# Linear attention's chunks placed between the key-block steps of the prompt attention, its exponents summed by TensorE

## The reference, cut to what matters

```python
def _fox_prompt(q, k, v, logf):            # prompt attention
    c = cumsum(logf)
    s = q @ k.T * scale + c[t] - c[s]       # causal
    return softmax(s) @ v

def _gla_chunk(S, inp):                     # one chunk of L tokens
    q, k, v, g = inp                        # g = log of the gates
    b = cumsum(g, axis=1)
    o_inter = (q * exp(b)) @ S
    A[t, s] = sum_k q[t, k] * k[s, k] * exp(b[t, k] - b[s, k])   # s <= t
    o = o_inter + A @ v
    S_new = exp(b_last) * S + (k * exp(b_last - b)).T @ v
```

## Time and profile before

| what | us |
|---|---|
| median of 3 runs (3704.17 to 3709.93) | 3708.62 |
| profiled execution, its own time | 3711.19 |
| its span, first to last instruction | 3709.5 |
| `fox_prompt` from its first instruction to the loop | 773.17 to 799.38 |
| `fox_prompt`'s loop | 799.4 to 1333.0 |
| `gla`'s first instruction, `merge`'s first | 1464.66, 1768.90 |

### The profile page before, as it was taken

The page is one execution under the profiler, slowest core; times in us unless marked ns, Lnnn a source line. Parts: engine busy times, 40 slices in busy tenths (PEclk is TensorE's granted clock), DMA queues, the critical chain, the costliest instruction groups (busy, mean ns, idle before and its releaser), DMA issues. The chain is left out here.

```text
span 3709.5 us, 47795 instructions
## 1 busy us (share of the span) xinstructions
PE 3229.8 (87%) x17920; PEld 2840.7 (77%) x17920; DVE 2089.8 (56%) x3141; ACT 835.2 (23%) x1455; POOL 649.7 (18%) x379
## 2 busy tenths in 40 slices
PE   5999999749999966566699699999998799999996
PEld 5999999625555535455477599999998699999995
DVE  5001112264444424798333378778776677787786
ACT  5111111223333311222222211111112211111112
POOL 0000000021212000565000322222223122222220
PEclk9999999869999978678799799999999799999997
DMA  4223121132221061222444411111112311111112
GB/s 108 69 69 113 54 69 51 32 83 52 47 57 41 12 186 60 65 76 63 127 143 129 125 46 45 45 49 47 45 45 89 113 46 45 45 45 45 51 39 87
DMA packets 246611, 255.76 MB, mean 69 GB/s; under 512 B 38009, under 2 KB 207369, under 8 KB 240289
## 3 DMA queue, kind: packets, MB, share of 16 engines
q1 hardware_dynamic: 245193, 250.42, 23.4%
q10 hardware_dynamic: 1344, 4.36, 0.5%
HBM read 187.82 MB, written 66.92 MB: 69 GB/s over the span
## 5 line engine op out<-in xcount | busy, mean ns | idle before, releaser
L2086 PE MATMUL ps_ffn<-h,wsp_n 128*128 128x312 f32 (+1 forms) x6336 | 1057.6, 323 | 42.1 <-POOL h L1922 28.6
L2086 PEld LDWEIGHTS ps_ffn<-h,wsp_n 128*128 128x128 f32 x6336 | 1018.4, 189 | 48.3 <-issue 37.6
L2021 DVE TENSOR_TENSOR yacc<-ps_ffn,yacc 128x312 f32<-128x312 f32 (+1 forms) x1056 | 495.1, 514 | 222.2 <-PE ps_ffn L2101 222.2
L391 PE MATMUL ps_project<-hT,wsp 128*128 128x416 f32 x3000 | 580.1, 354 | 3.2 <-DVE wsp L335 3.2
L391 PEld LDWEIGHTS ps_project<-hT,wsp 128*128 128x128 f32 x3000 | 562.1, 189 | 12.0 <-issue 5.0
L2101 PE MATMUL ps_ffn<-aT,dsp 128*128 128x312 f32 (+1 forms) x3168 | 545.0, 321 | 9.0 <-DVE yacc L2021 9.0
L2101 PEld LDWEIGHTS ps_ffn<-aT,dsp 128*128 128x128 f32 x3168 | 508.5, 188 | 11.7 <-issue 8.9
L1917 POOL TENSOR_TENSOR wsp_n<-wraw_n,wsp_n 128x1024 fp32r<-128x1024 f32 x88 | 210.5, 2392 | 801.9 <-ACT wsp_n L1958 801.9
L2035 DVE RECIPROCAL silu<-silu 128x416 f32<-128x416 f32 x132 | 306.2, 2320 | 4.5
L833 PE MATMUL ps_fox<-pexp,va 128*65 128x512 f32 (+3 forms) x640 | 295.6, 544 | 5.4 <-ACT pexp L880 5.4
L1988 ACT ACTIVATE aT<-a 128x416 fp32r<-128x416 f32 x132 | 65.2, 494 | 1004.1 <-DVE a L2043 1004.1
(11 more groups left out here) (222 smaller groups left out, 3125.0 us busy)
## 6 DMA issues: line engine op xcount, KB each, us to landing
wraw_n<-in_w_gate_dram SPq DMA_DIRECT2D x44, 512.0 KB, 3.8
wraw_n<-in_w_up_dram SPq DMA_DIRECT2D x44, 512.0 KB, 3.8
draw<-in_w_down_dram SPq DMA_DIRECT2D x44, 512.0 KB, 3.6
qk_raw<-zT SPq DMA_DIRECT2D x32, 512.0 KB
zT<-zs SPq DMA_DIRECT2D x12, 1040.0 KB
wraw<-in_w_in_dram SPq DMA_DIRECT2D x24, 512.0 KB
x<-x2s SPq DMA_DIRECT2D x20, 416.0 KB
h2T<-hT_m SPq DMA_DIRECT2D x20, 416.0 KB
```

The costliest lines, as they stand in the source:

```text
L391: last = pe.matmul(ps[:, g, 0:BLK], wsp[:, b, s, k, :], hT[:, g * TPB:(g + 1) * TPB, v, k, :], start=m == 0, stop=m == 3 * KD - 1)
L2021: dve.tensor_tensor(y, ps[:, 4 + i, 0:FB[b] * TT], y, ALU.add).then_inc(added, 1)
L2086: last = pe.matmul(ps[:, 2 * q + s, 0:FB[b] * TT], wsp[:, par, s, w, k, :], h2[:, FB0[b]:FB0[b + 1], v, k, :], start=m == 0, stop=m == 3 * ...
```

## The change

The stage `gla` goes. Its work on the 17 chunks moves into the prompt attention's stage, now `attend`, and none of it stays on GpSimd except masks.

- `gates` keeps the tokens on the partitions: nine pairs of chunks of 128 tokens by 256 channels (the bias comes in with a row of ones). It makes no running sums. The logarithms are stored in a high and a low fp32r part, `glog`, 4.2 MB where `gsum` had 2.1 MB.
- The exponents of all levels are matmuls: `gh`, the loaded logarithms, against `within`, a constant matrix of zeros and ones that GpSimd builds in `attend` before anything else of it can run (42 mask selects where `gla` had 14).
- A chunk's work is cut into steps r = 0 to 21 (`chunk_step` of each engine) and put behind the attention's step of the same number: chunk c starts at step 19(c-1) (`PERIOD`, `due`), so the 16 prompt chunks take up 304 of the 320 steps and a few more. The sample chunk (c = 0, padded to 128 rows) runs before the first step, and with it the first unit's maxima.
- The chunks take two of the eight PSUM banks (`GA`, `GO`). The maxima get two single banks where they had two pairs: `runs` lists them by 512 columns, 4, 8, 12 and 16 for G = 0 to 3, in the same steps as before.
- The loads and stores of a chunk (9 DMAs) are on the sync queue between those of the attention.

```diff
-            sp.wait_ge(sums, 4)
-            sp.dma_start(d["gsum"].rearrange("(g p) t -> p g t", p=P), run[:, 0:2, :]).then_inc(stored, 16)
-            sp.wait_ge(stored, 16 * 7)
+            sp.wait_ge(g_low, 2)
+            sp.dma_start(d["glog"][0:SEQ].rearrange("(c p) v k -> p c v k", p=P), parts[:, 0:NCH].bitcast(F32)).then_inc(stored, 16)
+            sp.dma_start(d["glog"][SEQ:NTOK], parts[0:NEW, NCH].bitcast(F32)).then_inc(stored, 16)
...
+            for n, part in ((P, slice(0, NCH)), (NEW, slice(NCH, NCH + 1))):
+                dve.tensor_tensor(neg[0:n, part], neg[0:n, part], pos[0:n, part], ALU.subtract).then_inc(sums, 1)
+            for k, (n, part) in enumerate(((P, slice(0, NCH)), (NEW, slice(NCH, NCH + 1)))):
+                dve.wait_ge(sums, k + 2)
+                dve.tensor_copy(parts[0:n, part, HI], neg[0:n, part]).then_inc(g_high, 1)
+                dve.wait_ge(g_high, k + 1)
+                dve.tensor_tensor(parts[0:n, part, LO], neg[0:n, part], parts[0:n, part, HI].bitcast(F32),
+                                  ALU.subtract).then_inc(g_low, 1)
...
-MX, ST, OB = 0, 4, 6
+MX, ST, OB, GA, GO = 0, 2, 4, 6, 7
...
                 if at >= 2:
                     pe.wait_ge(topped, at - 1)
-                for c in range(c0, min(c0 + 2, G + 1)):
-                    w = width(u, k, c)
-                    bank = MX + 2 * (at % 2) + c - c0
-                    last = pe.matmul(ps[:, bank, 0:w], qm[:, b, i * P:(i + 1) * P], km[:, b, 512 * c:512 * c + w],
-                                     start=True, stop=c < G)
-                    if c == G:
-                        last = pe.matmul(ps[:, bank, w - P:w], ident16[:], mask16[:], start=False, stop=True)
+                w = width(u, k, c)
+                bank = MX + at % 2
+                last = pe.matmul(ps[:, bank, 0:w], qm[:, b, i * P:(i + 1) * P], km[:, b, 512 * c:512 * c + w],
+                                 start=True, stop=c < G)
+                if c == G:
+                    last = pe.matmul(ps[:, bank, w - P:w], ident16[:], mask16[:], start=False, stop=True)
...
-def pairs(u):
-
-    return [(k, c) for k in range(NG) for c in range(0, group(u) + 1, 2)]
+def runs(u):
+
+    return [(k, c) for k in range(NG) for c in range(group(u) + 1)]
...
+PERIOD = 19
+NCHUNK = NCH + 1
+NSUM, NLEV, NPICK = 5, 5, NL + 2
+
+
+def due(s):
+
+    return [(c, s - PERIOD * (c - 1)) for c in range(1, NCHUNK) if 0 <= s - PERIOD * (c - 1) < PERIOD + 3]
...
+            def chunk_step(c, r):
+                if r == 5 and c + 1 < NCHUNK:
+                    load_gh(c + 1)
+                if r == 15 and c + 1 < NCHUNK:
+                    load_k(c + 1)
+                if r == 18 and c + 1 < NCHUNK:
+                    load_v(c + 1)
+                if r == 20:
+                    store_chunk(c)
+                    if c + 1 < NCHUNK:
+                        load_s(c + 1)
...
+            def sums(c, i):
+
+                if i == 0:
+                    pe.wait_ge(gh_come, 16 * (c + 1))
+                    if c == 0:
+                        pe.wait_ge(ready, 1)
+                    else:
+                        pe.wait_ge(ov_out, c)
+                elif i == 1:
+                    if c:
+                        pe.wait_ge(st_new, GH * c)
+                else:
+                    pe.wait_ge(ex_done, NSUM * c + i - 1)
+                bank = (GO, GA)[i % 2]
+                if i < 4:
+                    g, l0 = i % 2, 4 * (i // 2)
+                    for v in range(2):
+                        last = pe.matmul(ps[:, bank, :], gh[:, v, g * P:(g + 1) * P], within[:, l0:l0 + 4], start=v == 0, stop=v == 1)
+                else:
+                    for g in range(2):
+                        for v in range(2):
+                            last = pe.matmul(ps[:, bank, g * CH:(g + 1) * CH], gh[:, v, g * P:(g + 1) * P], within[:, E_K],
+                                             start=v == 0, stop=v == 1)
+                last.then_inc(sums_done, 1)
...
+            def levels(c, l0):
+
+                if l0 < 4:
+                    pe.wait_ge(ex_done, NSUM * c + (4, 5)[l0 // 2])
+                else:
+                    pe.wait_ge(picked, NPICK * c + l0 - 2)
+                for l in range(l0, min(l0 + 2, NL)):
+                    pe.wait_ge(keyed, NL * c + l + 1)
+                    for g in range(2):
+                        last = pe.matmul(place(l)[:, g * CH:(g + 1) * CH], ke[:, l, g, :], qe[:, l, g].rearrange("p e t -> p (e t)"),
+                                         start=True, stop=True)
...
+            def mixed(c, g):
+                if g == 0:
+                    pe.wait_ge(kdt_out, c + 1)
+                    pe.wait_ge(picked, NPICK * (c + 1))
+                    pe.wait_ge(qd_done, c + 1)
+                    pe.wait_ge(vl_come, 16 * (c + 1))
+                    if c < 2:
+                        pe.wait_ge(st_set, c + 1)
+                    else:
+                        pe.wait_ge(st_new, GH * c)
+                pe.matmul(ps[:, GO, g * 256:(g + 1) * 256], qd[:, g, :], st[:, g].rearrange("p e v -> p (e v)"), start=True, stop=False)
+                for h in (2 * g, 2 * g + 1):
+                    last = pe.matmul(ps[:, GO, h * GV:(h + 1) * GV], att[:, h, :], vl[:, h * GV:(h + 1) * GV], start=False, stop=h % 2 == 1)
+                if g:
+                    last.then_inc(o_done, 1)
+
...
+            def chunk_step(c, r):
+                if r < NSUM:
+                    sums(c, r)
+                if r in (6, 8, 10, 12):
+                    levels(c, r - 6)
+                if r == 14:
+                    diagonal(c)
+                if r in (16, 17):
+                    mixed(c, r - 16)
+                if r == 17:
+                    outer(c)
+
+            for r in range(PERIOD):
+                chunk_step(0, r)
+                if r == 10:
+                    for n in range(len(runs(0))):
+                        top_scores(0, n)
+                if r == 14:
+                    turn_tops(0)
             score(0, 0)
...
+                    for c, r in due(block0(u) + j):
+                        chunk_step(c, r)
...
+            def decay(c, i):
+
+                act.wait_ge(sums_done, NSUM * c + i + 1)
+                if c:
...
+                bank = (GO, GA)[i % 2]
+                if i < 4:
+                    out, by = ex[:, 4 * (i // 2):4 * (i // 2) + 4, i % 2, :], ps[:, bank, :].rearrange("p (l t) -> p l t", t=CH)
+                else:
+                    out, by = ex[:, E_K], ps[:, bank, 0:2 * CH].rearrange("p (g t) -> p g t", t=CH)
+                act.activation(out, by, ACT.Exp, scale=1.0 / TEMP).then_inc(ex_done, 1)
...
+                if u == 0:
+                    dve.wait_ge(st_stored, 32)
+                    dve.memset(st[:], 0.0).then_inc(st_set, 1)
...
+            def factors(c, l):
+
+                half = HALVES[l]
+                dve.wait_ge(ex_done, NSUM * c + (2 if l < 4 else 4))
+                dve.wait_ge(k_come, 64 * (c + 1))
+                if c:
+                    dve.wait_ge(level_done, NLEV * (c - 1) + l // 2 + 1)
+                by = halved(ex[:, l], half)
+                dve.tensor_tensor(halved(ke[:, l], half)[:, :, :, 0, :], halved(kr[:], half)[:, :, :, 0, :], by[:, :, :, 0, :], ALU.mult)
+                for e in range(2):
+                    rows = slice(e * GK, (e + 1) * GK)
+                    last = dve.tensor_tensor(qe[rows, l, :, e].rearrange("p g (n h) -> p g n h", h=half),
+                                             halved(qu[rows], half)[:, :, :, 1, :], by[rows, :, :, 1, :], ALU.mult)
+                last.then_inc(keyed, 1)
...
+            def chunk_step(c, r):
+                if r in (3, 4, 5):
+                    factors(c, 2 * (r - 3))
+                    factors(c, 2 * (r - 3) + 1)
+                if r == 6:
+                    factors(c, NL - 1)
+                    ends(c)
+                if 7 <= r < 7 + NL:
+                    pick(c, r - 7)
+                if r == 15:
+                    pick(c, NL)
+                    pick(c, NL + 1)
+                if r == 18:
+                    state(c)
+                if r == 19:
+                    gate(c)
+
```

More of the change, by code:

```diff
@@ L434 @@
 CH = 128
+NCH = SEQ // CH
+NPAIR = NCH // 2 + 1
 PJ = PAST // P
@@ L527, in _ @@
             pe.wait_ge(z_in, 32)
-            for g in range(2):
-                for b in range(NB):
-                    if g:
-                        pe.wait_ge(soft, 1 + b + 1)
-                    pe.matmul(ps[:, b, 0:BLK], wg2[:, g * P:(g + 1) * P], gg[:, b * BLK:(b + 1) * BLK],
-                              start=True, stop=True).then_inc(gate_done, 1)
-            pe.wait_ge(filled, 7)
+            for k in range(NPAIR):
+                n, cs, gate = pair(k)
+                if k >= NB:
+                    pe.wait_ge(soft, k - NB + 1)
+                for i, c in enumerate(cs):
```

(34 more changed lines are left out.)

703 lines of the change are left out of this document (308 added, 395 removed).

## The result

| | before | changed |
|---|---|---|
| median of the runs | 3709.27 us (3704.17 to 3713.73, 4 runs) | 3658.26 us (3657.52 to 3659.46, 4 runs) |
| profiled execution, span | 3709.5 us | 3657.7 us |
| mean granted clock | 0.933 | 0.944 |

The ratio is 0.9863, with a 95% interval of 0.9846 to 0.988: 51 us faster, where 112 were forecast. The table compares the two traces by pieces, each between two instructions that both have.

What follows compares the result with a forecast made beforehand. TensorE was taken to bound the prompt attention, VectorE `gla`. The profiled sum 3711.2 - 304.2 + 155 + 10 + 28 + 0 = 3600, with the median 2.6 us lower, gave 3597 us; range 3530 to 3670.

Steps and rivals of the forecast that it cites:

- the overlap: Loop and start: VectorE's chunk work fits under TensorE's except in G = 0; GpSimd's first splitting ends inside the sample chain.
- Removed, 304.2 us: Stage `gla`, from its first instruction to `merge`'s first, goes entirely: -304.2 us.
- TensorE's chunk work, 155 us: Attention loop: 9.7 us of TensorE at full clock for each of 16 prompt chunks, 155 us.
- VectorE's chunk work at 14.0 us: Each chunk: factors 6.0, `ends`, picks, state and gate on VectorE, together 14.0 us, 0.74 for each step.
- Pacing, +10 us: Attention loop: VectorE's waits in G = 0 and G = 1 and lumps elsewhere add 1.5 to 2 us a head.
- does VectorE stay under TensorE?: Loop, by unit: busy sums make VectorE the longer only in G = 0, 9.6 against 9.2 us.
- The start, +28 us: Ahead of the first score: mask building and sample chunk move it from 26.2 to about 49 us, plus a 5 us wait.
- `gates`, 0: Stage `gates`: scans removed (8.87 us), new work and a doubled store taken as equal, between -5 and +8.
- VectorE paces the loop: Rival: VectorE's chunk work and added maxima come on top of G = 0 to 2, loop +216, kernel 3648 us; chance 0.22.
- The half clock: Rival: stops in maxima-heavy units lower the whole loop's clock to 0.75, kernel 3782 us; chance 0.07.
- Idle absorbs it: Rival: TensorE's 31 us idle in the loop take chunk work, pacing costs nothing, kernel 3556 us; chance 0.13.
- no overlap: Rival: chunks run in series between the loop's steps, as long as in `gla`, kernel about 3740 us; chance 0.03.

Runs made afterwards that it cites:

- the two windows above: Loop profiles of two kernels: the change without its 16 prompt chunks (3463.49 us), and the change with GpSimd splitting only 64 columns from head 2 on (3620.48 us).
- the last kernel: Moved waits, early masks, second state tile, plus GpSimd making the constant rows and splitting head 0 after the sample chunk's factors and ends: 3602.66 us, ratio 0.9723.
- the short split: The change, but from head 2 on GpSimd casts and subtracts only 64 of a head's 2048 columns: 3620.48 us, ratio 0.977.
- the version with moved waits: The change, with GpSimd's splitting from head 1 on waiting for VectorE's factors of the chunk in hand, raw rows loaded ten steps later: 3625.36 us, ratio 0.9783.
- fills: The change, but from head 2 on GpSimd's four splitting instructions of a head replaced by memsets of the same tiles: 3623.22 us, ratio 0.9773.

## Why the prediction was wrong, and where it was right

The forecast of 3597 us named the right direction and missed the size: 51 us were gained where 112 were forecast. The measured time is in the range, 61 us above the value. The step that failed is the overlap: that VectorE's chunk work and GpSimd's splitting run beside each other, each in its own time, in the loop and ahead of the first score. The runs showed VectorE's products standing still until GpSimd's reading instructions had ended, 40 us of the loop.

- **Removed, 304.2 us: right.** Nothing of `gla` is left, and the stages on both sides kept their lengths (within 2 us each).
- **TensorE's chunk work, 155 us: right.** 152.7 between the two windows above. The mixed pricing (0.12 for 128 columns, 0.23 for 512) held.
- **VectorE's chunk work at 14.0 us: somewhat high, and no bound of what it can cost.** Between the two windows above VectorE's busy time is 437.8 - 243.4 = 194.4 us, 12.2 a chunk; the changed kernel's 480 us met the forecast only because its stops made up for it. A level's three undisturbed products take 0.82 us (they start at 790.57 and 791.39 in the last kernel), so a chunk's factors 5.7 us, forecast 6.0; of the three only the second starts before the one ahead has ended (790.78, against 790.86), and the next level's first waits for the last (791.39, against 791.36), so 14 of the 21 don't overlap, as the prediction had it. The differences from which I priced them hardly met GpSimd: in the turn of the earlier trace rows it stands idle beside them, and only five of the 112 ran under its reading instructions, 0.48 us each. The stage's other rows had stops in them (the 6.35 us above), and I took means without asking what ran beside them.
- **Pacing, +10 us: the term that failed.** With the short split the added waits are 11.1 (single banks; I had +1 a head in G = 1, 8 us, for this crowding) + 7 (TensorE's idle time) = 18; with the splitting 40.4 more. The step "does VectorE stay under TensorE?" added up VectorE's work by unit and set it against TensorE's. GpSimd's column stood beside them in the earlier trace rows (8.23 us in G = 0, 4.56 in G = 2), and all I had said of GpSimd is that no chunk work stays on it. What I didn't ask is what kind of instruction moves beside the one that stays. The old loop's VectorE read its scores from PSUM; the new one multiplies SBUF by SBUF. Two smaller faults are in the same comparison. The added maxima of G = 1 and G = 2 are exchanged (a unit makes those of the next: four more in G = 1, eight more in G = 2, so +0.6 and +1.2). And G = 2 is TensorE's by its sums (25.3 against 20.7), while 7.8 us of VectorE's 19.6 came back there: sums over a unit don't show the waits within it.
- **The start, +28 us: 38 measured**, and the same step failed there: I let GpSimd's splitting run "inside" the sample chunk's chain (39 against 49 us after the stage's start). It ran there, but it held the chain's factors from 799.5 to 808.8. The stop on the state's store, forecast at about 5, was 7.66 us on TensorE (5.58 on VectorE).
- **`gates`, 0: right** (+1.1).
- **Rivals.** "VectorE paces the loop" gave +216 us for the loop and 3648 for the kernel, nearer to the measured +211 and 3658 than the forecast. That is luck; its mechanism, chunk work on top of the units of G = 0 to 2, was not what happened: with the splitting out of the way the loop is 171 us longer than before, the forecast's 165 and not the rival's 216. A number that fits isn't a mechanism; only the short split told them apart. The half clock came in single units (0.54 for 15 us behind the longest stop), for 15 us in all on TensorE's busy time (658.6 against 643.5), and not in the loop (0.95). "Idle absorbs it" and "no overlap" have nothing for them.

What stays open: how the waits that are left divide between the two engines, and whether waits can be placed so that the whole splitting meets neither products nor negations.

## What to carry to other kernels

Before work is moved under another stage, put the operands beside the engines, not only the busy times: here a VectorE instruction with two operands in SBUF, and a small negation with one, stood until GpSimd's reading instruction had ended (products of 0.29 us took up to 4.57, negations of 0.17 up to 4.21). A helper that costs nothing today costs what stands behind the VectorE instruction that it stops. In a trace, such a meeting shows as a few instructions of 2 to 6 us among hundreds of 0.3, so look at the longest of a group and at the units that differ from their like, not at the mean. Place the helper behind the other's work with a semaphore that is there already, and then look at what it meets in its new place: it gave most of the short split's gain and put negations in its way. Cutting it in pieces gave half.

## What the runs showed of the hardware that I had not expected

The stop lasts as long as GpSimd's instruction, not a share of it: a product of 0.29 us ended 0.15 us after a subtraction of 4.49 us, and the two stops of a line of 6.55 us lie behind two GpSimd instructions back to back. In the same stretches VectorE's reductions and casts out of PSUM kept their times, as did the predicated copies from PSUM, and so did GpSimd's own instruction (4.49 to 4.64 us with a product waiting, 4.49 to 4.56 without), so in this loop all of the cost is on VectorE.

Two inputs in SBUF are not the only case. The negation has one, and took 4.21 and 3.67 us in the version with moved waits and in the last one; a reduction of 16 columns in SBUF just ahead of it kept its 0.16 us. The last kernel has one ahead of the first score too, ending at 805.59 with GpSimd's subtraction (805.56):

```profile
804.49 1.10 DVE L1249 TENSOR_SCALAR ntop<-top 128x4 f32<-128x4 f32 x1
```

The trace of the kernel before has such a negation as well, 1.07 us at 793.51, beside the splitting of head 0; with the product of 6.35 us it was the hint that I passed over. Whether fills hold a negation back, no run shows.

The cost in the kernel (40.4 us) was more than the stopped time (34 us): 25 of it are TensorE's idle time, and 15 its busy time, since it came back from the longer stops at half clock.
